# The last down weights loaded after pass 8's products, and the token tiles' output writes held for the late gathers

## The reference, cut to what matters

```
x = x + mixer(rmsnorm(x, norm1_g))
u = rmsnorm(x, norm2_g)
combine = top 2 experts of the 4 in the top group, softmax weights     # 16 experts
h = silu(u @ w_gate[e]) * (u @ w_up[e])                                # 256 wide
x = x + sum over e of combine[e] * (h @ w_down[e])
y = rmsnorm(x, final_norm_g)
```

## Time and profile before

| | us |
|---|---|
| median of 3 runs | 811.86 |
| lowest and highest | 811.46, 812.39 |
| the profiled execution | 810.71 |
| its span in the profile | 809.1 |
| PE busy | 778.9 (96%) |
| DVE busy | 432.6 (53%) |
| ACT busy | 210.9 (26%) |
| DMA, mean | 157 GB/s |

### The profile page before, as it was taken

How to read it: one execution, slowest core, us unless ns; L and a number is a source line. 1 busy time by engine, 2 the same in 40 slices (tenths; PEclk the granted TensorE clock), 3 DMA queues, 4 the chain that set the end, 5 groups by cost and what they waited for, 6 DMA issues and landing times.

```text
span 809.1 us, 19993 instructions
## 1 busy us (share of the span) xinstructions
PE 778.9 (96%) x8538; PEld 537.7 (66%) x8538; DVE 432.6 (53%) x855; ACT 210.9 (26%) x497; POOL 39.2 (5%) x50
## 2 busy tenths in 40 slices
PE   7999999999999999999999999999999879999994
PEld 5877777787767877777777877767788633333331
DVE  5965567688768565657666555346204431111144
ACT  4122222254523312221212232220022411111153
POOL 0000000000000000000000000000000011221211
PEclk9999999999999999999999999999999879999997
DMA  9541422432112101201230112065835679999964
GB/s 332 209 156 49 134 94 80 157 105 85 71 53 80 53 28 56 68 15 58 72 118 28 35 49 80 3 225 206 354 132 197 244 290 408 393 394 389 369 237 180
DMA packets 36678, 127.19 MB, mean 157 GB/s; under 512 B 5827, under 2 KB 16099, under 8 KB 31728
## 3 DMA queue, kind: packets, MB, share of 16 engines
q1 hardware_dynamic: 32560, 115.78, 38.2%
q0 software_dynamic: 4032, 10.15, 4.3%
HBM read 106.83 MB, written 18.68 MB: 155 GB/s over the span
## 4 chain that ended last, share of the span: by engine, by line
PE 89%; DVE 4%; DMA 3%; issue 2%; ACT 0%; POOL 0%; SPq 0%; POOLq 0%; DVEq 0%; ACTq 0%
PE psum L1370 23%; PE psum L1351 12%; PE psum L1703 10%; PE psum L2614 9%; PE psum L2648 4%; PE psum L1328 4%; DVE arena L2050 2%; PE psum L1315 2%; PE psum L1571 2%; PE psum L1303 2%; DMA arena<-x_rows,ids 2%; PE psum L1659 1%; PE psum L1584 1%; PE psum L2594 1%; PE psum L1468 1%
## 5 line engine op out<-in xcount | busy, mean ns | idle before, releaser
L2050 DVE TENSOR_TENSOR arena<-arena 128x268 f32<-128x268 f32 (+10 forms) x322 | 175.3, 544 | 48.9 <-ACT arena L1802 29.8
L1370 PE MATMUL psum<-arena 128*128 128x268 f32 x784 | 189.5, 393 | 0.0
L1370 PEld LDWEIGHTS psum<-arena 128*128 128x128 f32 x784 | 145.4, 190 | 37.6 <-issue 11.6
L1802 ACT ACTIVATE arena<-psum 128x268 f32<-128x268 f32 (+7 forms) x215 | 85.5, 405 | 276.8 <-PE psum L1370 146.6
L2050 DVE TENSOR_TENSOR arena<-psum,arena 128x256 f32<-128x256 f32 (+5 forms) x170 | 71.8, 426 | 80.7 <-PE psum L1584 21.8
L1351 PE MATMUL psum<-arena 128*128 128x268 f32 x392 | 105.0, 403 | 0.0
L1703 PE MATMUL psum<-arena 128*128 128x268 f32 x384 | 91.0, 391 | 1.6 <-DVE arena L2050 1.2
L2614 PE MATMUL psum<-arena 128*32 128x512 f32 (+1 forms) x640 | 86.8, 606 | 0.5 <-DVE arena L2771 0.3
L1351 PEld LDWEIGHTS psum<-arena 128*128 128x128 f32 x392 | 69.9, 189 | 20.3 <-issue 6.3
L1703 PEld LDWEIGHTS psum<-arena 128*128 128x128 f32 x384 | 71.2, 189 | 17.5 <-issue 3.3
L2771 DVE TENSOR_TENSOR arena<-psum,arena 128x256 f32<-128x256 f32 (+2 forms) x38 | 24.3, 663 | 101.8 <-ACT arena L2683 90.8
(11 more groups left out here) (210 smaller groups left out, 701.5 us busy)
## 6 DMA issues: line engine op xcount, KB each, us to landing
arena<-in_w_gu SPq DMA_DIRECT2D x16, 2048.0 KB, 19.7
arena<-in_w_in SPq DMA_DIRECT2D x45, 512.0 KB, 4.3
arena<-in_w_dn SPq DMA_DIRECT2D x16, 1024.0 KB, 18.1
arena<-in_w_out SPq DMA_DIRECT2D x2, 2048.0 KB, 14.1
arena<-arena SPq DMA_DIRECT2D x5, 536.0 KB, 5.6
arena<-in_x SPq DMA_DIRECT2D x8, 268.0 KB, 5.4
arena<-arena SPq DMA_DIRECT2D x16, 134.0 KB, 4.4
arena<-in_x SPq DMA_DIRECT2D x1, 2144.0 KB, 14.5
```

What stands on the lines that cost most here:

```text
L1370: last = mm(ps, w[:, k, :], x[:, k, :], start=(k == 0 and i in (0, 1, 3)), stop=(k == KD // 2 - 1), skip_group_check=i not in (0, 1, 3))
L1802: run(nc.scalar.activation(out, in_, fn, **kw), s)
L2050: run(v.tensor_tensor(out, a, b, op), s)
```

## The change

Two edits on SP's queue, and none elsewhere. The load of expert 15's down weights is issued in the loop with the others, when the products of pass 8 are done (`q_dn` at least 9), ahead of the waits for the adds and the scatter; the old wait there (for pass 7, with no load behind it) is replaced. And a wait for the three late gathers (`z_in` at least 48) stands before the first of the output writes, where the load was.

```diff
@@ -2508,16 +2508,15 @@
                         if i > NWE:
-                            at_least(sp, q_dn, DOWNS, last_pass(i - 1 - NWE) + 1)
-                            if i < NE:
-                                load_dn(sp, i - 1)
+                            at_least(sp, q_dn, DOWNS, last_pass(i - 1 - NWE) + 1 if i < NE else SUMS + 1)
+                            load_dn(sp, i - 1)
                     for q in range(2):
                         at_least(sp, q_yd[q], ADDS[q], ADDS[q])
                         sp.nop(nofuse=True)
                     for t in TILES:
                         n = rows_of(t)
                         sp.dma_start(xf[0:n, t, :], x2_dram[t * P:t * P + n, :]).then_inc(z_x[t], 16)
-                    load_dn(sp, NE - 1)
+                    at_least(sp, z_in, 16 * LATE, 16 * LATE)
                     for j, t in enumerate(TILES):
                         at_least(sp, z_y, TT + LATE, j + 1)
                         sp.nop(nofuse=True)
```

## The result

The changed kernel is slower, not faster. Its median over 22 runs is 813.82 us, against 811.46 for the kernel before on the same chips; the ratio is 1.0029 with a 95% interval of 1.0018 to 1.0040, which is 2.4 us. 809.9 was forecast, and 811.9 was the end of the range. A second series gave 1.0031 (1.0016 to 1.0046). The executions of the changed kernel lie between 810.8 and 816.4 us, those of the kernel before between 808.7 and 813.0. One run of 1596 us, of which there is no trace, is left out of the ratio; without it the changed kernel's median is 813.60.

What follows compares the result with a forecast made beforehand. The late gathers were taken to set the end, with PE's last product next. A gain of 2.2 us less 0.35 for the scatter's delay gave 1.9, so 809.9 us against the median of 811.86; range 809.2 to 811.9.

Steps and rivals of the forecast that it cites:

- the tail that I ran forward: End of the kernel, with gathers done at 788: `summed(0)` waits for PE until 789.8; 2.2 us less.
- Part three: Load at 770 beside pass 8's scatter: scatter lands 0 to 1.9 us later, 0.5 taken, costing 0.35 us.
- the sum of work: DMA engines, 770 to 776: 1.9 us of work plus 2.55 for the load, 4.4 of 6 us.
- The row of the 29.3 us: Profile row: load of expert 14's down weights, issued at 746.7, landed 29.3 us later, at 776.0.
- What a delay costs: Scatter to reads, ACT's squares, `hidden(11)` and PE: 0.5 us late costs 0.35, 1.9 costs 1.75.
- Part four: Held output writes at the end: done about 793, the fifth at 796.8 to 798.7, not pushing POOL's second scatter.
- Part one: Late gathers, without the load and writes beside them: third lands at 788 instead of 792.6.
- the load takes the scatter's turn: Rival at pass 8's scatter: it lands 7.8 us later, kernel 5.4 us slower, 817.3; chance 0.08.
- its point of decision: Scatter delay from which the slower rival decides: 2.4 us, and 4 to be seen.
- Its price of 5.4 us: Slower rival's loss: 7.6 - 2.2 us, with the scatter delayed as the adds of passes 2 to 7 were.
- The partial gain: Rival: scatter loses 1 to 2 us or gathers land at 790.5 to 791.5; gain 0.2 to 1.5 us; chance 0.24.

Runs made afterwards that it cites:

- e3: Changed kernel with the early load cut from 1 MB to 64 KB; 809.49 us, ratio 0.9980 to the kernel before.
- e12: Changed kernel as it is, run again for a second trace; 814.69 us, ratio 1.0031 to the kernel before.
- e6: Changed kernel with the load issued at 758, when pass 7's products are done, writes held; 812.74 us, ratio 1.0028 to the kernel before.
- e1: Kernel before with only the load moved to 770, output writes not held; 813.26 us, ratio 1.0030 to the kernel before.
- e2: Kernel before with only the output writes held for the late gathers, load left behind the five reads; 810.06 us, ratio 0.9991.
- e7: Kernel before with the load issued once the third of five reads has landed, and writes held; 809.72 us, ratio 0.9983.
- e5: Kernel before with the load issued behind the wait for the late gathers, ahead of the output writes; 811.65 us, ratio 1.0008.
- e8: Changed kernel with the preceding load, expert 14's down weights, cut to 64 KB; 809.42 us, ratio 0.9979 to the kernel before.
- e9: Changed kernel with three token tiles instead of four ahead of pass 11's gate on ACT; 810.80 us, ratio 1.0002 to the kernel before.
- e4: Kernel before with the load issued behind the waits for adds and scatter, ahead of the five reads, writes held; 814.67 us, ratio 1.0043.

## Why the prediction was wrong

**What bounded the kernel: right.** The late gathers set the end, and a gain there is worth no more than PE's last product allows; e3 has the tail that I ran forward, with `summed(0)` waiting for PE. 2.2 us were forecast for it, 1.6 to 1.7 measured.

**Part three failed: the scatter's delay beside the load.** I took 0.5 us for the scatter's delay, with 1.9 as the most. It was 3.3 in the profiled execution, and about 2 in the mildest traces with the full load beside it (6.2 against 4.2). Even the bound was too low. I put the load behind the old one on the engines that still had work, 776.0 + 2.55 = 778.6, and left out the scatter's own rows, which have to go through the same engines. With 0.52 MB at 412 GB/s for them, 1.3 us, it would be 779.9, close to the 780.1 of the load and the 780.26 of the scatter; but that sum is made afterwards, and POOL's queue moved only some 0.3 MB from 774 on, so the closeness proves nothing. I had argued that the sum of work, 4.4 of 6 us, fits. It fits on the average of sixteen engines. A transfer has landed when its last part has: 0.19 MB of loads and 0.08 MB in the scatter's queue were still to go at 776, and took 4 us. The row of the 29.3 us had hinted at it, with a load that landed 6 us after the engines had become mostly idle.

**What a delay costs: named rightly, priced too low.** The order of links was as I had it: scatter, reads, four squares, `hidden(11)`, PE. Three things were missing in the price. Issuing the reads took 1.0 us more (3.22 instead of 2.19; 3.44 in e12 and 3.04 in e6). The later reads landed more slowly (the third 7.5 us from its issue instead of 4.8, the fourth 7.9 instead of 6.8, the fifth 10.0 instead of 9.1; in e1, with its scatter of 6.2 us, they did not). And PE, once idle for 4.65 us, ran `down(10)` at the lower clock, for 2.0 us more. By the trace: `down(11)` starts 30.6 us behind the end of `down(8)` instead of 23.9, 6.7 us late: 0.36 in the wait for `u_rows`, which is not the load's doing, 4.65 in the wait for `hidden(11)`, 2.2 in `hidden_in(11)` and `down(10)`, less the 0.44 that `down(11)` stood for the gathers before. The tail behind it is 1.9 us shorter, since DVE is not late any more. 6.7 - 1.9 is the 4.8 us of the stretch. This accounts for one execution of 815.68 us, and not for the median.

**Part four, the writes: right for the changed kernel, with less room than I gave them.** They went out in one burst, the fifth behind its norm, and POOL's first scatter did not push the second. In e2 and e7 it did: it took 2.0 us instead of 1.0, the second went out directly behind it (802.65 and 802.50), and the chain that ended last runs over the fifth write. Nothing was lost by it, as the third scatter still came 1.17 us behind the last norm; in e5 1.3 us were. **Part one: right in size.** The third gather went from 12.36 us to 8.4 in e3 and 9.4 in the change.

**The rivals.** What happened is the slower one, "the load takes the scatter's turn", to which I gave 0.08: the mechanism holds, and so does its point of decision (2.4 us of delay), as far as the traces of the change (3.3 us, slower) and of e8 (2 us, not slower) go. Its price of 5.4 us was taken from the adds, for a delay of 7.8 us, and is more than twice the median's loss; that the profiled execution lost 4.8, with a delay of 3.3, is near it by luck. The chance was too small because it rested on part three's bound of 1.9 us. The partial gain, 0.24, is the same mechanism with less delay. The Trainium skill, "DMA: Bandwidth & Descriptors", section "Queues, rings and completion order", says that engines take turns between queues, and from that I had estimated 1.3 us as the scatter's most; the trace's 3.3 is beyond it. The estimate spread the rows evenly over sixteen engines, which the trace contradicts; whether the engines take turns no run here shows.

**What stays open.** Why a few of the DMA engines lag, how the scatter's delay splits between old and new loads, and why one of SP's read issues stood (the third in the changed kernel and e12, the fifth in e6). The clocks under e12 suggest that the lower clock goes with the upper part of the changed kernel's spread; how much of the median's loss it is was not tried by itself.

## What to carry to other kernels

Before a transfer is moved into a stretch where the DMA engines look idle on average, look up when the last transfer issued before it lands. Here that was at the end of a stretch of 6 us at 0.31 of their time, and the moved transfer took 9.5 us in it, and the scatter beside it 3.3 us more than before. Follow a moved load to what shares the engines with it, and give the short chain that leads back to PE more cover than the delay may be; one tile less ahead of PE's last input (e9) did away with the loss, though not with the delay that cost the gain. And a transfer held back has a latest time, too: e5 won at the gathers and lost the same at the weights and the output writes.

## What the runs showed of the hardware

Three things were not expected. A 64 KB load issued behind others on the same queue landed after 28.7 us (e8), and one issued at 772.2, when of SP's loads only that of 748.7 was still out, landed after 5.4 us, at 777.7, just behind the old one at 777.3 (e3).

The granted clock was at its lower level when PE came back from a stall of 2.18 us (e6), 3.86 (e12) and 4.65 (changed), and in e4 it fell within 1 us of the end of a stall of 3.26; `down(10)` took 4.9, 6.01, 5.66 and 5.35 us; after 0.57 and 0.61 us (e1, e8) it was at the upper one, and `down(10)` took the 3.66 us of before.

And the stretch ahead of the change is not the same from one execution to the next: the end of `down(8)` lies between 769.9 and 772.2 us in the 12 traces that have the same instructions before it, so two spans can't be compared to better than 2.3 us. The stretch from a common point can be compared more closely, here to the 0 to 0.8 us that PE waits for `u_rows` behind it.
